# Norm of the heads begun inside the window attention, its spread over four banks beside an unsplit first output product

## The reference, cut to what matters

```
ada = silu(c) @ w_ada + b_ada            # six vectors of 1024: shift, scale, gate, twice
h = rms_norm(x, norm1_g) * (1 + scale1) + shift1
q, k, v, b, c, u = split(h @ w_in + b_in)
attn = head_rms_norm(sliding_window_sink_attention(q, k, v, sinks), attn_out_g)   # 8 heads of 64
conv = head_rms_norm(b * conv3(c * u), conv_out_g)                                # 8 groups of 64
x = x + gate1 * (concat(attn, conv) @ w_out + b_out)
h2 = rms_norm(x, norm2_g) * (1 + scale2) + shift2
x = x + gate2 * peer_layer(h2, ...)      # then the final norm, and a second block of two layers
```

## Time and profile before

| what | value |
|---|---|
| median of three runs | 3417.79 us |
| the profiled execution | 3427.08 us, its span 3425.3 us |
| PE busy | 3320.0 us (97%) |
| DVE, ACT, POOL busy | 1866.2, 806.1, 1939.3 us |
| mean granted clock of PE | 0.986 of full speed |

### The profile page before, as it was taken

The page is one execution under the profiler, slowest core; times in us unless marked ns, Lnnn a source line. Parts: engine busy times, 40 slices in busy tenths (PEclk is TensorE's granted clock), DMA queues, the critical chain, the costliest instruction groups (busy, mean ns, idle before and its releaser), DMA issues. The chain is left out here.

```text
span 3425.3 us, 44439 instructions
## 1 busy us (share of the span) xinstructions
PE 3320.0 (97%) x15228; PEld 2656.6 (78%) x15228; DVE 1866.2 (54%) x3082; ACT 806.1 (24%) x1384; POOL 1939.3 (57%) x1154
## 2 busy tenths in 40 slices
PE   6989999999999999999999999999999999899999
PEld 4756888888888878888888666688877887588876
DVE  7742458586785657777777333322116788323205
ACT  2322212121212111111111243322114554222103
POOL 5424664645555566676667422466656665366664
PEclk9989999999999999999999999999999999999999
DMA  7412333636353475555555211222222111122232
GB/s 283 163 46 80 104 133 107 240 104 230 117 209 130 171 272 193 191 195 195 193 189 183 75 49 37 74 98 98 99 80 86 62 62 50 62 92 98 98 100 72
DMA packets 141180, 438.33 MB, mean 128 GB/s; under 512 B 13600, under 2 KB 13728, under 8 KB 136864
## 3 DMA queue, kind: packets, MB, share of 16 engines
q1 hardware_dynamic: 82544, 301.62, 25.6%
q10 hardware_dynamic: 58544, 135.55, 11.4%
HBM read 367.91 MB, written 69.21 MB: 128 GB/s over the span
## 5 line engine op out<-in xcount | busy, mean ns | idle before, releaser
L2202 POOL TENSOR_SCALAR whi<-ring 128x1024 fp32r<-128x1024 f32 x511 | 556.8, 1090 | 1428.4 <-issue 680.5
L2204 POOL TENSOR_TENSOR wlo<-ring,whi 128x1024 fp32r<-128x1024 f32 x511 | 1299.6, 2543 | 42.7
L436 PE MATMUL ps<-norm_hi,whi 128*128 128x512 f32 x1288 | 550.5, 427 | 2.9 <-POOL wlo L2204 1.7
L438 PE MATMUL ps<-norm_hi,wlo 128*128 128x512 f32 x1288 | 505.0, 392 | 0.0
L437 PE MATMUL ps<-norm_lo,whi 128*128 128x512 f32 x1288 | 503.3, 391 | 0.0
L436 PE MATMUL ps<-mixed_hi,whi 128*128 128x512 f32 x1024 | 399.1, 390 | 2.7 <-DVE mixed_lo L1895 2.7
L437 PE MATMUL ps<-mixed_lo,whi 128*128 128x512 f32 x1024 | 399.0, 390 | 0.0
L438 PE MATMUL ps<-mixed_hi,wlo 128*128 128x512 f32 x1024 | 398.9, 390 | 0.0
L1891 DVE TENSOR_TENSOR A<-A 128x512 f32<-128x512 f32 x128 | 354.0, 2765 | 20.8 <-DMA A<-gate_map 20.2
L436 PE MATMUL ps<-mix_hi,whi 128*128 128x512 f32 x752 | 294.5, 392 | 0.0
L437 PE MATMUL ps<-mix_lo,whi 128*128 128x512 f32 x752 | 293.5, 390 | 0.0
(11 more groups left out here) (337 smaller groups left out, 5227.5 us busy)
## 6 DMA issues: line engine op xcount, KB each, us to landing
ring<-stream SPq DMA_DIRECT2D x519, 512.0 KB, 3.3
gelu_map<-A ACTq DMA_DIRECT2D x128, 256.0 KB, 2.0
gate_map<-A ACTq DMA_DIRECT2D x16, 2048.0 KB, 11.4
A<-gelu_map ACTq DMA_DIRECT2D x128, 256.0 KB, 3.3
A<-gate_map ACTq DMA_DIRECT2D x32, 1024.0 KB, 6.0
A<-ada_w SPq DMA_DIRECT2D x10, 2048.0 KB, 7.9
A<-ada_w SPq DMA_DIRECT2D x4, 1024.0 KB, 22.7
X<-x_in SPq DMA_DIRECT2D x1, 2048.0 KB, 19.0
```

The lines of the kernel that those rows point to most:

```text
L436: first = mm(out_, lh, rh, start=start, stop=False)
L438: return first, mm(out_, ll, rh, start=False, stop=stop)
L2202: g.tensor_scalar(h[:], raw[:], 1.0, 0.0, ALU.mult, ALU.add).then_inc(whi_ready, 1)
L2204: g.tensor_tensor(rest[:], raw[:], h[:].bitcast(F32), ALU.subtract).then_inc(split_ready, 1)
```

## The change

- PE sums the squares of the heads in the order 0, 1, 4, 5, 6, 2, 3, 7 (planes 0 to 3 are attention, 4 to 7 convolution), the first four ahead of unit 7's first `in_part`, the others behind unit 7; the sums go to bank 7. ACT makes the first four squares in unit 6 behind the exponentials of unit 7, then in unit 7 the table load for the root and the square of plane 6 ahead of the copy of unit 7's output, and the last three behind that copy.
- The spreads go to four banks instead of two. `w_out` becomes a stage with an unsplit first product: three spreads, then one matmul of the unsplit product and one spread in turn. DVE scales all eight planes, then makes all low parts.
- Modulation group 11 is loaded into other planes, behind the last convolution, accumulated between the residuals of `w_out`; `ada_columns(5)` and `ada_take(5)` go behind `w_out`. The rows of group 11 and `ada_columns(5)` leave unit 6 and the place ahead of the sums of the heads.
- At the start SP loads x ahead of group 1, PE runs the sums of norm1 ahead of `ada_columns(0)`, and DVE the reciprocal of norm1 ahead of `ada_take(0)` and group 3.

```diff
@@ PE
-        RELEASED = ("w_in", "w_query", "dqkv", "ffn_in0", "ple_gate0", "ffn_in1", "ple_gate1")
+        RELEASED = ("w_in", "w_out", "w_query", "dqkv", "ffn_in0", "ple_gate0", "ffn_in1", "ple_gate1")
...
+        HEADS_ORDER = (0, 1, 4, 5, 6, 2, 3, 7)
+        HEADS_EARLY = 4
...
+            def head_sums(i0, i1):
+                for i in range(i0, i1):
+                    c, j = NSQ["heads"] + i, HEADS_ORDER[i]
+                    pe.wait_ge(sq_ready, c + 1)
+                    mm(ps[0:32, 7, :], pick_halves[:, 28 - 4 * j:60 - 4 * j], plane(NORM["heads"][0] + c % 4),
+                       start=i == 0, stop=i == KC - 1).then_inc(sq_used, 1)
...
+            sums("norm1")
             ada_columns(0)
-            sums("norm1")
             ada_columns(1)
...
+                if u == UNITS - 1:
+                    pe.wait_ge(ada_ready, 5)
+                    head_sums(0, HEADS_EARLY)
                 in_part(*fill_groups(u, 0))
...
+            head_sums(HEADS_EARLY, KC)
+            release(PROD["w_in"] + 19)
+            for j in range(3):
+                spread(j)
+            for k in range(KC):
+                unsplit("w_out", lambda k: pe.wait_ge(scaled_ready, SCALED["heads"] + k + 1),
+                        lambda k: plane(MIX + k), k, k + 1)
+                if k + 3 < KC:
+                    spread(k + 3)
+            linear("w_out", "mix", begun=True)
+            release(PROD["w_out"] + 8)
             ada_columns(5)
-            sums("heads")
-            spread("heads")
+            sums("norm2")
             pe.wait_ge(ada_ready, 6)
-            linear("w_out", "mix")
-            release(PROD["w_out"] + 8)
-            sums("norm2")
@@ ACT, in win_extra(u)
+                if u == UNITS - 2:
+                    act.wait_ge(o_taken, TB)
+                    head_squares(0, HEADS_EARLY)
+                if u == UNITS - 1:
+                    fn(early_root[:, g:g + 1], ones[:, 0:1], ACT.Sqrt)
+                    head_squares(HEADS_EARLY, HEADS_EARLY + 1)
@@ DVE
             for g in range(3):
                 ada_accumulate(g)
+            inverse("norm1")
             ada_take(0)
             ada_accumulate(3)
-            inverse("norm1")
...
-                if u % 2 == 0:
+                if u in (0, 2, 4):
                     ada_accumulate(8 + u // 2)
...
                 v.scalar_tensor_tensor(out=X[:, j, :], in0=plane(PQ + j), scalar=ada_col(GATE1, j), in1=X[:, j, :],
                                        op0=ALU.mult, op1=ALU.add).then_inc(residual_ready, 1)
+                if 1 <= j < 5:
+                    ada_accumulate(11, j - 1, j)
+            ada_take(5)
@@ SP
             load_ada(0)
+            sp.dma_start(X[:], x_in).then_inc(x_loaded, 16)
             load_ada(1)
-            sp.dma_start(X[:], x_in).then_inc(x_loaded, 16)
...
-            ada_behind = {5: 6, 6: 7, 9: 8, 12: 9, 15: 10, 18: 11}
+            ada_behind = {5: 6, 6: 7, 9: 8, 12: 9, 15: 10, 22: 11}
...
+                    if g == 11:
+                        sp.wait_ge(conv_ready, 4)
                     load_ada(g)
-            refills(FIRST["w_out"] + RING, FIRST["w_query"] + RING)
+            refill_unsplit("w_out")
+            refills(FIRST["w_out"] + RING + 1, FIRST["w_query"] + RING)
```

More of the change, by code:

```diff
@@ L284, in ada_col @@
             return ada[:, part + j:part + j + n]
[L287 removed]
+        ADA_FIRST, ADA_RING, ADA_LAST, ADA_END, ADA_SUMS = 24, 44, 52, 32, (60, 62, 16, 18, 20, 22)
         ADA_HALVES = (2, 3)
         def ada_planes(g):
[L292 removed]
+            first = ADA_FIRST + 8 * g if g < 4 else ADA_RING + 8 * (g % 2) if g < 8 else ADA_LAST if g < 11 else ADA_END
             return A[:, first:first + 8, :].rearrange("p (k a) t -> p k (a t)", a=2)
@@ L480, in linear, with some @@
                 per = body * 8 // pad
-                def some(t0, p0, i, np_, released=False):
+                def some(t0, p0, i, np_, released=False, first=True):
                     for q in range(np_):
@@ L485, in some @@
                         if q == 0 and released:
-                            unsplit(name, ready, whole)
+                            if first:
+                                unsplit(name, ready, whole)
                             continue
@@ L521, in linear @@
                     if name in RELEASED:
-                        some(t0, p0, 0, per, released=True)
+                        some(t0, p0, 0, per, released=True, first=not begun)
                     with pe.Fori(int(name in RELEASED), loops) as i:
@@ L540, in sums, with spread @@
                     pe.wait_ge(root_ready, g - 1)
-                for j in range(k):
+                for j in range(k) if name not in PACKED else ():
                     c = NSQ[name] + j
                     pe.wait_ge(sq_ready, c + 1)
[L544 to L556, removed]
+                    mm(ps[:, 2 + g % 2, :], ones[:], plane(NORM[name][0] + c % 4), start=j == 0, stop=j == k - 1)\
+                        .then_inc(sq_used, 1)
+            def head_sums(i0, i1):
[4 more added lines that the diff above has]
+                       start=i == 0, stop=i == KC - 1).then_inc(sq_used, 1)
+            def spread(j):
+                pe.wait_ge(rstd_ready, NUMBER["heads"] + 1)
+                if j >= 4:
+                    pe.wait_ge(scaled_ready, SCALED["heads"] + j - 3)
+                mm(ps[:, 4 + j % 4, :], spread_halves[:, j, :], A[0:32, NORM["heads"][1], :], start=True, stop=True)\
+                    .then_inc(spread_ready, 1)
             def spread_rstd(name):
@@ L1096, in root @@
                     rows = slice(0, 32 if name in PACKED else P)
-                    fn(A[rows, NORM[name][1], :], ps[rows, 2 + g % 2, :], ACT.Sqrt, scale=1.0 / width,
+                    fn(A[rows, NORM[name][1], :], ps[rows, 7, :], ACT.Sqrt, scale=1.0 / width,
                        bias=eps_col[eps][rows]).then_inc(root_ready, 1)
@@ L1182, in win_early, with head_squares @@
                     take_in(j)
+            def head_squares(i0, i1):
+                for i in range(i0, i1):
+                    c, j = NSQ["heads"] + i, HEADS_ORDER[i]
+                    if i >= 4:
+                        act.wait_ge(sq_used, c - 3)
+                    if j >= 4:
+                        act.wait_ge(conv_ready, j - 3)
+                    fn(plane(NORM["heads"][0] + c % 4), plane(ATT + j) if j < 4 else zv[:, j - 4, 2:T + 2],
+                       ACT.Square).then_inc(sq_ready, 1)
             def win_extra(u):
@@ L1602, in ada_accumulate @@
                 total = ada_partial(part)
-                if g % 2:
+                if g % 2 and k0 == 0:
                     dve.wait_ge(ada_used, g)
-                for k in range(4):
+                for k in range(k0, k1):
                     dve.wait_ge(*ada_signal(g, k))
@@ L1717, in _ @@
             dve.wait_ge(conv_ready, 4)
-            behind(KC, lambda j: scaled("heads", j, plane(ATT + j) if j < 4 else zv[:, j - 4, 2:T + 2],
-                                        par[:, COL["attn_out_g"] + j:COL["attn_out_g"] + j + 1], plane(MIX + j)),
-                   lambda j: low("mix", j, plane(MIX + j)))
+            for j in range(KC):
+                scaled("heads", j, plane(ATT + j) if j < 4 else zv[:, j - 4, 2:T + 2],
+                       par[:, COL["attn_out_g"] + j:COL["attn_out_g"] + j + 1], plane(MIX + j))
+            for j in range(KC):
+                low("mix", j, plane(MIX + j))
             dve.wait_ge(ada_ready, 3)
@@ L2346, in _ @@
             done = FIRST["keys"] + RING + 2
-            for name in UNSPLIT[2:]:
+            for name in UNSPLIT[3:]:
                 refills(done, FIRST[name] + RING)
```

14 lines of the change are left out of this document (7 added, 7 removed).

## The result

| | median of the runs, us | lowest to highest | runs |
|---|---|---|---|
| before | 3425.46 | 3414.09 to 3427.45 | 20 |
| after | 3428.09 | 3425.87 to 3430.55 | 20 |

The ratio after/before is 1.0016, with an interval of 1.001 to 1.0023: some 5 us slower, less than the 0.2% that the forecast named as the least that can be told, yet outside the forecast's range of 3407 to 3424 in absolute time. The three times of before that the forecast started from (3417.52 to 3423.13) lay low among the twenty: that alone moves the base up by 7.7 us. The profiled execution of after took 3430.55, its span is 3428.8 against 3425.3, so **+3.5**, where -1.2 was forecast.

What follows compares the result with a forecast made beforehand. The prediction took PE, busy 97% of the span, as the bound. Its terms +3.2, -10.1, +5.3 and +0.4 summed to -1.2 us, taking the median from 3417.79 to 3416.6 us, range 3407 to 3424.

Steps and rivals of the forecast that it cites:

- The start: Kernel start: x loads before group 1, DVE's groups end later, first scaling moves from 40.63 to 43.8: +3.2 us.
- Rival 3: Kernel start: the exchanged loads cost nothing, sum -4.4, 3413.4 us; chance only within the 0.72 of the near cases.
- Units 6 and 7: Units 6 and 7 to the late sums' end: the wait for probabilities goes, sums end earlier: -10.1 us.
- rivals 2 and 4: PE's clock falls from unit 7's entry, sum +8.8, chance 0.09; DVE's wait returns as wait for squares, at most 2 us.
- Root, spreads and first product: First spread through first product of `w_out`: half clock up to the last spread, 24.8 against 19.45: +5.3 us.
- rival 1: Pairs of unsplit matmul and spread: full clock returns inside them, -3.3 instead of +5.3, 3408.0 us; chance 0.16.
- Behind `w_out`: After `w_out`, ahead of norm2's sums: `ada_columns(5)` takes 1.84 where PE stood 1.48: +0.4 us, bounds 0 to 2.

Runs made afterwards that it cites:

- experiment 3: The changed kernel with the start order of the kernel before (group 1 loaded ahead of x): 3420.42 us, ratio to before 0.9993.
- 1: The changed kernel with the first product of `w_out` split again, eight spreads back to back: 3421.97 us, ratio to before 1.0000.
- 7: The changed kernel with zero-padded 128-row spreads back to back, split first product, old start and `ada_columns(5)` behind the sums of norm2: 3409.59 us, ratio to before 0.9963.
- 12: The changed kernel with all eight sums of the heads behind unit 7, none ahead of it: 3430.0 us, ratio to before 1.0024.
- 5: The changed kernel, pairs kept, with spreads padded by zeros from 32 to 128 rows: 3412.48 us, ratio to before 0.9965.
- 6: The changed kernel with four filling 128-row matmuls in the pause before the first spread, spreads still 32 rows: 3416.11 us, ratio to before 0.9985.
- 2: The changed kernel with blocks of four spreads and four unsplit matmuls instead of pairs: 3417.19 us, ratio to before 0.9984.
- 11: The kernel before with only its spreads padded by zeros to 128 rows: 3416.54 us, ratio to before 0.9984.
- 4: The changed kernel with `ada_columns(5)` behind the sums of norm2 and `ada_take(5)` behind the reciprocal: 3424.42 us, ratio to before 1.0002.
- 15: The kernel before, unchanged, traced once more in one execution: 3417.68 us.
- 16: The changed kernel, unchanged, timed in more rounds and traced again: 3426.43 us over 12 runs, ratio to before 1.001.

## Why the prediction was wrong

**The start (+3.2) was right**: +2.6 at the scaling, +2.8 at unit 7. Group 1 was what DVE waited for, `ada_columns(1)` fell to half clock as worked out, and experiment 3 gives 2.2 of it back. Rival 3 is out.

**Units 6 and 7 (-10.1) were right in size** (-10.05), and so were the stations: no wait for the probabilities, 0.35 us for the first square where 0.75 was said, and full clock through both pauses, so that rivals 2 and 4 are out. Experiments 1 and 7 show that POOL's split in unit 6 is worth 2.7 us of it as a wait (3.0 instead of 0.35), with 1.7 us of half clock behind it, and 12 that the early sums are worth nothing.

**Root, spreads and first product (+5.3) is the step that failed: +8.3.** The clock was read rightly, at 0.50 up to the last spread, and rival 1 is out. What failed is the sentence "At half clock an fp32 matmul of 512 columns takes 1.71 to 1.75, with 32 rows (14.02 / 8) as with 128 (twice the 0.86)". Both prices come from rows where like follows like. In the pairs each matmul follows one with another row count and starts 2.00 us behind it. There are eleven such changes: the ten steps from 213.36 to 233.39 take 20.0 us where 17.1 was forecast, and the three spreads ahead of them 5.4 instead of 5.1. That is 3.2 us; 0.2 came back behind the last change, which leaves the missing 3.0. The number stood in the stretch of the earlier trace rows, whose next two lines on PE's timeline are these:

```profile
2090.39 1.65 PE L849 MATMUL ps<-A 128*128 128x384 f32 x2
2091.97 1.65 PE L851 MATMUL ps<-A 64*128 64x384 f32 x2
```

The starts are 1.58 apart (2088.81, 2090.39, 2091.97), where 384 columns at the 1.71 for 512 would be 1.28: 0.30 on top, at a change between 128 and 64 rows. The forecast used these rows for the clock and passed over the beat. Experiments 5 and 6 show that the row count is the cause, and the weight loads where the time goes.

The forecast said too little about how much lay in this step. It took half clock as given and asked whether the pairs would end it. Experiments 2, 5 and 11 show that it ends in 5 us where the matmuls have 128 rows, that is for a write of zeros on DVE, which has time for it.

**Behind `w_out` (+0.4) became +2.4.** That is outside the bounds of 0 to 2 that were given. 1.7 of it is the clock's fall behind the one-column matmuls, which is in one of the two traces of after, and 0.6 is that these matmuls with their pause of 0.30 take 2.1 us ahead of the sums where PE had stood for 1.48. Moved behind the sums, as in 4, they delay nothing, though half of what `w_query` gains is lost in its first product.

**The base.** With the right sum the forecast would have been 3417.79 + 3.5 = 3421.3, inside the range, and the measured median 3428.09 still outside: 7.7 of the 11.5 us between forecast and median are the base, for which the working had no term. Three runs of a kernel whose executions lie between 3414 and 3427 did not fix its median to better than that. (The upper end of the range was also not what its own reasons give: 3416.6 with 1.8 more for the start, 3.0 for the late sums and 1 for the clock's phase is 3422.4, not 3424.) The sum was made against one execution of 3427.08, 9.3 us above that median, and the text carried a difference over without asking why the two lay so far apart. Both kernels' times are governed by where the clock falls, and a range of the absolute time has to hold that. After's median stands 2.6 us above before's where the ratio says 5.5: the twenty runs of before are spread over 13 us and unevenly (their mean is 3422.9, their median 3425.46), and such a median says little to a few microseconds.

**The rule of the Trainium skill** that was weighed, sustained activity of TensorE releases the throttle ("TensorE: Matmul & The Clock Gate", Part 1, The HAM clock gate), fails here for spreads of 32 rows (0.50 for 13.9 us) and holds for 128 (1.00 after 5.3 us): see 11. The forecast took the trace's side for the spreads, and that was right.

**What stays open.** Whether it is the share of 32-row work or the pauses at each change that keeps the clock down inside the pairs was not separated: 11 shows that rows alone can do it in spreads without pauses, and 6 that the mix with pauses does not bring it down. Why the fall at norm2 comes in one execution and not in the next is open too, as is why the clock falls at other places behind `w_query` from one execution of the same kernel to the next.

## What to carry to other kernels

Behind a pause, look at how many rows the next matmuls have before counting how many there are: padding a 32-row operand with zeros to 128 rows took 4.8 us off S in the kernel before and 13.7 in the kernel after, for no added TensorE time. Don't let matmuls of different row counts take turns; in blocks of four the same work was 9.8 us shorter. And where a kernel's own runs are spread over 13 us, ask where in that spread the profile and the base lie before a term of 3 us is argued.

## What the runs showed of the hardware

- A change of row count (32 and 128) between consecutive fp32 matmuls costs 0.29 to 0.30 us at the granted clock 0.50 and 0.20 us at 1.00; the weight load then starts only with its own matmul (213.36 and 215.36 in after). The same 0.30 stands between 128 and 64 rows of 384 columns (1.58 instead of 1.28).
- 32-row matmuls back to back for 13.9 us leave the granted clock at 0.50, 128-row ones of the same number and width have it at 1.00 after 5.3 us (11). Once it is at 1.00 right ahead of them, it stays there under 32-row and 128-row matmuls in turn for 16 us (6); behind the pause of 4.21 it fell even where the first 0.6 us of the 32-row spreads had still been at 1.00 (15).
- An instruction of DVE over 128x4 takes 2.35 to 2.36 us beside POOL's tensor operation of 2.37 us (before, 1, 7, 11), and 0.16 where POOL does none (after).
- Behind sixteen one-column matmuls (1.92 us) that follow a pause of 0.30, the granted clock went to 0.50 under the 512-column sums in five of eight traces (after, 1, 3, 6, 12, and not in 2, 5, 16), and in none of the ten in which the one-column matmuls did not stand ahead of the sums.
